# Spreading the decay rows of a hybrid GDN and attention block over the partitions: a transfer through DRAM in place of matrix products

## What is computed

```python
def reference(x, ...):
    h = _rmsnorm(x, norm1_w[l])
    proj = h @ w_in[l]
    gq, gk, gv, gz, gb, ga, aq, ak, av = jnp.split(proj, IN_SPLITS, axis=-1)
    qkv = jax.nn.silu(_causal_conv(jnp.concatenate([gq, gk, gv], axis=-1), conv_w[l]))
    beta = jax.nn.sigmoid(gb)
    g = -jnp.exp(a_log[l]) * jax.nn.softplus(ga + dt_bias[l])
    o_gdn = _gated_delta_rule(cq, ck, cv, g, beta)
    ...
    o_attn = _sliding_window_attention(aq, ak, av, sinks[l], q_norm_w[l], k_norm_w[l])
    x = x + jnp.concatenate([o_gdn, o_attn], axis=-1) @ w_out[l]
    h2 = _rmsnorm(x, norm2_w[l])
    x = x + jnp.square(jax.nn.relu(h2 @ w1[l])) @ w2[l]

def _gated_delta_rule(q, k, v, g, beta):
    gc = jnp.cumsum(g, axis=-1)
    decay = jnp.exp(jnp.where(incl, gc[..., :, None] - gc[..., None, :], -jnp.inf))
    a = jnp.where(strict, jnp.einsum('bhncd,bhnsd->bhncs', kb, k) * decay, 0.0)
    # two triangular solves with (a + 1), then a scan over the chunks
    ...
```

## Time and profile before

| | before |
|---|---|
| median of 3 runs | 2435.66 us |
| the profiled execution | 2435.2 us |
| its span, first to last instruction | 2433.6 us |
| mean granted TensorE clock | 0.999 of full speed |
| PE busy | 2382.2 us (98%) |
| DVE busy | 1412.4 us (58%) |
| ACT busy | 951.0 us (39%) |
| POOL busy | 147.2 us (6%) |
| DMA | 232.63 MB, mean 96 GB/s |

### The profile page before, as it was taken

The page is one execution under the profiler, slowest core; times in us unless marked ns, Lnnn a source line. Parts: engine busy times, 40 slices in busy tenths (PEclk is TensorE's granted clock), DMA queues, the critical chain, the costliest instruction groups (busy, mean ns, idle before and its releaser), DMA issues. The chain is left out here.

```text
span 2433.6 us, 36578 instructions
## 1 busy us (share of the span) xinstructions
PE 2382.2 (98%) x12718; PEld 1961.2 (81%) x12718; DVE 1412.4 (58%) x2096; ACT 951.0 (39%) x1697; POOL 147.2 (6%) x157
## 2 busy tenths in 40 slices
PE   5999999999999999999999999999999999999998
PEld 4888788888888878888888887888888888788886
DVE  6677663454668755245466866535556685643544
ACT  4466432223356633122335653212234664321222
POOL 0021000000003100000000300000000130000000
PEclk9999999999999999999999999999999999999999
DMA  4211222234321222224332122222432212222241
GB/s 148 97 63 54 96 95 95 95 111 144 104 92 53 71 95 96 95 95 140 111 104 87 53 79 93 97 95 95 142 119 94 78 45 96 92 99 95 95 146 70
DMA packets 63172, 232.63 MB, mean 96 GB/s; under 512 B 7361, under 2 KB 7361, under 8 KB 62401
## 3 DMA queue, kind: packets, MB, share of 16 engines
q1 hardware_dynamic: 55728, 202.64, 25.0%
q0 software_dynamic: 7312, 28.32, 3.3%
HBM read 222.54 MB, written 8.39 MB: 95 GB/s over the span
## 5 line engine op out<-in xcount | busy, mean ns | idle before, releaser
L1354 PE MATMUL ps<-h_h,w_h 128*128 128x512 f32 x2004 | 789.3, 394 | 16.0 <-DVE w_l L803 7.9
L1354 PE MATMUL ps<-h_h,w_l 128*128 128x512 f32 x2004 | 780.9, 390 | 0.0
L1354 PE MATMUL ps<-h_l,w_h 128*128 128x512 f32 x2004 | 780.8, 390 | 0.0
L803 DVE TENSOR_TENSOR w_l<-stage,w_h 128x1024 fp32r<-128x1024 f32 x381 | 466.7, 1225 | 274.5 <-ACT w_h L443 258.2
L443 ACT CAST w_h<-stage 128x1024 fp32r<-128x1024 f32 x381 | 398.5, 1046 | 552.1 <-PE ps L1354 543.9
L1354 PEld LDWEIGHTS ps<-h_h,w_h 128*128 128x128 f32 x2004 | 376.6, 188 | 111.6 <-DVE w_l L803 13.3
L1354 PEld LDWEIGHTS ps<-h_h,w_l 128*128 128x128 f32 x2004 | 376.6, 188 | 78.6
L1354 PEld LDWEIGHTS ps<-h_l,w_h 128*128 128x128 f32 x2004 | 376.9, 188 | 77.8 <-issue 1.9
L1354 PE MATMUL ps<-ff_h,w_h 128*128 128x512 f32 x1036 | 404.6, 391 | 0.0
L1354 PE MATMUL ps<-ff_h,w_l 128*128 128x512 f32 x1036 | 403.1, 389 | 0.0
L1354 PE MATMUL ps<-ff_l,w_h 128*128 128x512 f32 x1036 | 403.1, 389 | 0.0
(11 more groups left out here) (185 smaller groups left out, 1847.2 us busy)
## 6 DMA issues: line engine op xcount, KB each, us to landing
stage<-w SPq DMA_DIRECT2D x385, 512.0 KB, 3.3
x_next<-x POOLq DMA_DIRECT2D x20, 512.0 KB, 6.4
out<-xs POOLq DMA_DIRECT2D x32, 256.0 KB, 2.3
xs<-x POOLq DMA_DIRECT2D x8, 512.0 KB, 4.7
xs<-x POOLq DMA_DIRECT2D x4, 1024.0 KB, 5.4
bia<-bias POOLq DMA_DIRECT2D x1, 1024.0 KB, 5.0
cst<-con SPq DMA_DIRECT2D x1, 704.0 KB, 4.5
prm<-par SPq DMA_DIRECT2D x1, 39.5 KB, 1.9
```

What stands on the lines that cost most here:

```text
L803: dve.tensor_tensor(w_l[:, b, 0:k], stage[:, s, 0:k], w_h[:, b, 0:k].bitcast(F32), ALU.subtract).then_inc(w_lo.sem, 1)
L1354: return pe.matmul(o, a, b, start=start, stop=stop)
```

## The change

The selecting products and their constants go. After the scans, POOL writes the four partitions of `row` that hold the decay rows to a DRAM scratch `row_copy` of 4x512 (8 KB). It waits for that to land, and reads the scratch back once for each of the 128 partitions into a new SBUF tile `rowb` of 128x4x512 (8 KB on each partition, 1 MB in all), which lies over tiles that are free at this time. DVE and ACT read `rowb` where they read bank `ROW`. DVE waits for the transfer once per group, in `decay(0)`, and no longer for `p_gr`. PE drops its waits for `eg_r`.

```diff
-K_ID, K_ONE, K_MEAN, K_MEANX, K_HALF, K_CAUS, K_LEV, K_SEL = 0, 1, 2, 3, 4, 5, 6, 7
-N_CONST = K_SEL + HEADS
+K_ID, K_ONE, K_MEAN, K_MEANX, K_HALF, K_CAUS, K_LEV = 0, 1, 2, 3, 4, 5, 6
+N_CONST = K_LEV + 1
...
+        with ExitStack() as s:
+            rowb = sb("rowb", [P, HEADS, TOK], F32, s)
...
+        row_copy = nc.dram_tensor("row_copy", (HEADS, TOK), F32, kind="Internal").ap()
...
+        def row_tile(t):
+            return rowb[:, :, t * P:t * P + P]
...
+        row_saved = signal("row_saved", 1, step=16)
+        row_spread = signal("row_spread", 1, step=16)
...
+                pool.wait_ge(row_dve.sem, row_dve.after(g, row_dve.per_group))
+                pool.nop(nofuse=True)
+                pool.dma_start(row_copy, row[A4, :]).then_inc(row_saved.sem, 16)
+                pool.wait_ge(row_saved.sem, row_saved.after(g, 1))
+                pool.nop(nofuse=True)
+                pool.dma_start(rowb[:], row_copy.unsqueeze(0).to_broadcast([P, HEADS, TOK])).then_inc(row_spread.sem, 16)
...
-                    act.activation(eg[:, a], heads(ROW), ACT.Exp).then_inc(B["eg_r"].sem, 1)
+                    act.activation(eg[:, a], row_tile(t), ACT.Exp).then_inc(B["eg_r"].sem, 1)
...
-                    wt(B["p_gr"], t)
                     if t == 0:
+                        dve.wait_ge(row_spread.sem, row_spread.after(g, 1))
                         dve.wait_ge(xs_free.sem, xs_free.after(g, 0))
-                    dve.tensor_tensor(sm[:, t, DGC].unsqueeze(2), heads(ROW)[:, :, P - 1:P],
+                    dve.tensor_tensor(sm[:, t, DGC].unsqueeze(2), row_tile(t)[:, :, P - 1:P],
                                       sm[:, t, NB].unsqueeze(2), ALU.subtract)
-                    dve.tensor_tensor(d1[:, a], heads(ROW), per_head(cst[:, K_CAUS, :]),
+                    dve.tensor_tensor(d1[:, a], row_tile(t), per_head(cst[:, K_CAUS, :]),
                                       ALU.add).then_inc(B["d2"].sem, 1)
...
-                    tile, q, k = row[0:64, t * P:t * P + P], part(0, t), part(1, t)
-                    if t:
-                        wt(B["eg_r"], t - 1)
-                    four(heads(ROW), lambda o, h: mm(o, cst[0:64, K_SEL + h, :], tile), B["p_gr"])
+                    q, k = part(0, t), part(1, t)
...
-                    elif t == 1:
-                        wt(B["eg_r"], TILES - 1)
```

More of the change, by code:

```diff
@@ L166, in build @@
         tb = sb("tb", [P, 17 * BLOCK])
+        row_copy = nc.dram_tensor("row_copy", (HEADS, TOK), F32, kind="Internal").ap()
         ps = ctx.enter_context(nc.psum_tensor("ps", [P, 8, 512], F32))
         SC, PT, OV, NS, A0 = 0, 2, 3, 1, 6
-        GRAM, ROW, KQ = 4, 5, 0
+        GRAM, KQ = 4, 0
         VROW, KROW = 2, 3
@@ L310, in build @@
         B = {n: signal(n, TILES) for n in
-             ("p_gr p_gg p_kt p_vt p_kq p_ks p_vv p_oo p_su p_on "
+             ("p_gg p_kt p_vt p_kq p_ks p_vv p_oo p_su p_on "
               "d2 dg_r ssk bias_r dgc at_r qk_r vb_r kd_r res_r osq2 o1 o2 mlo "
@@ L1784, in constants @@
         c[:, K_LEV, 64 * l:64 * l + HD // 2] = (k[:, None] // (2 * b) == j[None, :] // (2 * b)) & (k[:, None] % (2 * b) >= b)
-    for h in range(HEADS):
-        c[32 + h, K_SEL + h] = 1.0
     q = i[:, None]
```

## The result

| | before | after |
|---|---|---|
| median | 2435.45 us (6 runs) | 2447.26 us (6 runs) |
| lowest to highest | 2434.24 to 2436.82 | 2444.24 to 2455.33 |
| ratio of the times | | 1.0052, interval 1.0042 to 1.0061 |
| the profiled execution | 2435.2 us | 2450.95 us |
| its span | 2433.6 us | 2449.4 us |

The change makes the kernel slower by 0.5%. The forecast was 0.4% faster, and 2447.26 us lies outside the range. The spread of the runs has grown too, from 2.6 to 11.1 us.

A forecast was written before the change was run, and what follows sets the result against it. PE was 98% busy, but an ACT/DVE chain nearly as long limited the gain to the smaller of both. 4 x (2.44 - 0.1) + 0.5 = 9.9 us off gave a 2425.8 us median, range 2423.5 to 2440.

The forecast's parts named there:

- the chain's gain: ACT/DVE chain in passes 1 to 3 and block inverse: idle times close, 1.74 + 0.70, 2.44 us per group.
- The smaller constants: Program start: constants shrink from 704 to 448 KB, so first weight unit lands sooner; 0.5 us, once.
- the other 2.0 us of PE's lead turn into a wait ahead of `masked`: After the passes: of PE's 4.4 us lead per group, 2.0 us become PE idle time ahead of `masked`.
- 0.1 us late: Row transfer per group: lands at 124.85 us as its 7.7 us cover ends; 0.1 us comes off the gain.
- a sign of being wrong: Profile after: the prediction is wrong if DVE stands in `decay(0)` for microseconds.
- POOL's start and the two waits: Row transfer after the scans: POOL's start and two waits, taken as 0.2 us.
- read back of 1 MB: Second transfer, DRAM to `rowb`: taken as 5.6 us, from 5.0 us alone and 5.4 us beside others.
- The fit of that page: Row transfer: 2.0 us plus bytes over 436 GB/s gives 2.0 and 4.4 us, nothing late, 0.4 us better.
- Late by 1.3 to 3.8 us: Case of the row landing 1.3 to 3.8 us late at `decay(0)`; chance 0.20.
- late, but not by more than the chain gains: Rival: row landing, say 2 us late, leaves 0.44 us per group, 2433.4 us; lateness of 1.3 to 3.8 us had 0.20.
- The slow rival: Rival: read back slow as 128 partitions read the same 8 KB, 5.2 us late, 2446.2 us; chance 0.18.
- PE alone decides: Rival: in the passes all of PE's 4.4 us per group comes off, 18 us, 2417.6 us; chance 0.05.

The follow-up runs named there:

- x1: Changed kernel with both transfers replaced by a POOL memset of `rowb` to a constant (decays wrong): 2435.59 us against 2435.64 before, ratio 1.0013.
- x6: Changed kernel with a memset of `rowb` for the transfers (decays wrong) and two 128x512 filling products ahead of `masked`: 2427.58 us, ratio 0.9962.
- x2: Changed kernel with each partition reading its own 8 KB from a constant 1 MB DRAM tensor (decays wrong): 2450.1 us, ratio 1.0063.
- x7: Changed kernel with write and read back in two parts, tile 0's first, then tiles 1 to 3: 2439.56 us, ratio 1.0022.
- x9: Changed kernel with the read back delayed by a POOL memset of `rowb` after the write, on another chip: 2437.74 us against 2436.94 before, ratio 1.0003.
- x5: Kernel before, with three DVE reductions holding back the scatter so PE idles ahead of `masked`: 2458.17 us against 2436.54, ratio 1.0098.
- x3: Changed kernel with the selecting products kept on PE, into their old bank that nobody reads: 2438.34 us, ratio 1.001.
- x4: Changed kernel with two 128x512 products by constants on PE ahead of `masked`, where it would be idle: 2438.55 us, ratio 1.001.
- x8: Changed kernel with the transfer in two parts and two filling products ahead of `masked`, whole computation in place: 2429.08 us, ratio 0.9969.

## Why the prediction was wrong

**Right: the chain's gain.** 2.44 us per group were forecast, and x1 measured 2.5 with the row in time. That the row in time and a steady clock give about the sum is shown by x6, 9.0 us off against 9.9. The smaller constants, taken as 0.5 us, gave nothing that the profile shows: they landed in 3.5 us in place of 4.5, yet the first scans ended at 117.24 us against 117.15.

**Wrong, and it decides: "the other 2.0 us of PE's lead turn into a wait ahead of `masked`", counted as free.** The wait came (1.6 us). What I did not ask is what PE's clock does behind an idle time. In five profiles with this wait of 1.56 to 1.61 us (after, x1, x2, x7, x9) the clock fell behind it in 11 of 20 groups; with 2.1 us (x5) in 4 of 4; in the five profiles where PE has work there or waits less than 1 us (before, x3, x4, x6, x8) in none of 20. A fall lasted 6.8 to 20.5 us. In the profiled execution of the change three falls account for 14.5 of the 15.8 us (8.71 + 2.43 + 3.36); between the medians, x4 against the change, it is 8.7 of 11.8 us. What stands behind `masked` are products of 64x32 and 64x128, with DVE and ACT waiting on them (in the window of group 1 above both fall with PE, from 13.40 and 11.54 us of work to 9.01 and 6.32). The Trainium skill (TensorE: Matmul & The Clock Gate, "HAM oscillation — how this bites in real kernels") describes a kernel in which PE's waits make it fall to its lower level and pay again each time; the runs here agree, down to a single wait of 1.6 us per group in a kernel that is 97% busy. The prediction named the clock nowhere, neither as a term nor as a rival.

**Wrong in size: the landing, "0.1 us late".** It was 1.95 to 3.22 us late, and DVE stood in `decay(0)` for 2.15 to 3.40 us, which the prediction had named as a sign of being wrong. The terms of my sum against the rows of after:

| term | taken | measured |
|---|---|---|
| POOL's start and the two waits | 0.2 | 1.1 (0.58 + 0.55) |
| write of 8 KB | 1.9 | 1.7 |
| read back of 1 MB | 5.6 | 6.8 to 8.0 |

The last one is the largest. I took it near the 5.4 us of a load "beside others", though the earlier trace rows showed the weight unit issued at 119.49 us, where my own sum put the read back; I had the unit just behind it, and it went 0.53 us ahead. Out of its way the read back took 5.0 us in place of 7.7 in the median (x9), and x2 shows that the repeated source costs nothing. I also gave 6.4 us as the median of four loads queued together. That is the median of all 20 loads of x; the four together had 7.7. The Trainium skill (DMA: Bandwidth & Descriptors, "Issuing engines are not separate DMA queues") says that transfers of all issuing engines run on the same 16 engines and interleave; the packets of the change and x9 agree, and so does the weight unit of 5.4 to 5.7 us in x7. The fit of that page, by which nothing would be late, does not hold for this place: it leaves the other stream out. What happened up to `masked` is what I gave 0.20, "Late by 1.3 to 3.8 us". It went past the rival "late, but not by more than the chain gains" in three groups: +1.1 us in all four together where the forecast had -9.4 (4 x 2.34).

**The slow rival** gave 2446.2 us, close to the 2447.26 measured, but for a wrong reason: its mechanism, the repeated source, is refuted by x2, and its lateness of 5.2 us did not come. That PE alone decides is refuted by x1, x6 and x8, where `masked` comes 2.2 to 2.5 and not 4.4 us sooner.

**What stays open.** Why the clock held behind the same wait of 1.6 us in nine of 20 groups (group 0 of the change and of x2, two groups of x1 and of x7, three of x9), and how long an idle time must be. The waits of 0.62 to 0.93 us in x3 went without a fall, and those of 1.93 us at the program's start fell in five of eleven. Earlier idle times may add to it: in the six groups in which PE had also stood idle for 0.9 to 1.2 us some 16 us behind the scans (groups 1 to 3 of the change and of x2) the clock fell in all six, in the other 14 in five. x9 is without that earlier wait, and without any filling its seven executions have mean clocks of 0.996 to 0.999, near those of before. But x1 and x7 are without it too, and have 0.986 to 0.994; and x9 ran on another chip. The places alone don't tell it either, since the runs of one kernel differ (x1: 2433.13 to 2450.82 us). Whether moving real work into the gap would do better than useless products was not tried.

## What to carry to other kernels

An idle time of PE is not free merely because another engine sets the pace: the clock may fall behind it and cost several times the wait (here 2.4 to 8.7 us for 1.6). So look at the granted clock behind each new idle time, and give PE work to do there, useless if need be. Cost a transfer at its place, with what else is on the DMA engines in the same microseconds, and count the start of the issuing engine and each wait, about 0.55 us here; if the first consumer needs only a part, send that part first. And a forecast of "the gain on one engine turns into a wait" is only half done until it says what that wait does.

## What the runs showed of the hardware

- One idle time of 1.6 us on PE took the granted clock from 1.00 to 0.50 in 11 of 20 cases, one of 2.1 us in 4 of 4; each fall lasted 6.8 to 20.5 us, and 2 us of products by constants in the gap kept it at 1.00 in all 12 groups where they stood.
- Large products behind the gap do not prevent it: behind 1.93 us at the program's start, ahead of products of 128x512, the clock fell in 5 of 11 profiles, for 3.4 us.
- A 1 MB read back took 7.7 us when a 512 KB weight unit had been issued 0.5 us ahead of it and the next 4.5 us behind, and 5.0 us when they were issued 2.5 us ahead and 2.5 us behind.
- 128 partitions reading the same 8 KB of DRAM were as fast as 128 reading their own (7.7 and 7.7 us, both beside the same weight units).
- A quarter of the bytes is not a quarter of the time: 256 KB in pieces of 512 bytes took 5.1 us where 1 MB took 7.7. Other transfers ran beside both, so how much of this is the size of the pieces is not shown.
- POOL issued a transfer 0.58 us behind the end of DVE's scans and about 0.55 us behind the landing of another transfer.
